# Gathering expert rows with one transfer per slot or with two, in a transformer kernel on one core

## Chip, core and metric

The kernel runs on 1 core of a Trainium2 chip. The metric is the device time of one execution in microseconds (us), taken as the median of several runs. Durations below come from one profiled execution; in the profile PE is TensorE's matmuls and PEld its weight loads, DVE is VectorE, ACT ScalarE, POOL GpSimd and SP SyncE.

## What is computed

The kernel computes two transformer blocks for 512 tokens of width 1024. The stage that matters is the expert layer of the first block. Each token picks 8 heads x 16 = 128 experts out of 16384; for each it takes a row of 1024 floats of a table u and one of a table v:

```python
ug = jnp.take(u_tab, idx, axis=0)
act = jax.nn.gelu(jnp.einsum('td,thkd->thk', xb, ug).astype(jnp.float32), approximate=False)
vg = jnp.take(v_tab, idx, axis=0)
return jnp.einsum('thk,thkd->td', (gate * act).astype(xb.dtype), vg)
```

Before it stand a recurrent mixer and the query projection, behind it a gated feed-forward, attention with a second mixer, and a second feed-forward. They are not touched.

## The kernel before, in words

The 512 tokens are 4 tiles (TT) of 128 tokens, one token per partition. One of a token's 128 chosen experts is a **slot**, so a tile has 128 slots and the layer 512. The work runs slot by slot through five engines, with a ring of 8 row buffers (GROUPS = 8); 8 slots are a round, and a tile has 16 rounds.

Before the change the two tables lie side by side as one table `peer_uv` of 16384 rows of 2048 floats (8 KB). For a slot:

1. GpSimd issues one indirect DMA (L2006) that fetches for each of the 128 tokens the 8 KB row that its expert index names: 1 MB, 128 rows. The indices come from a small tile `expert_ids`, which GpSimd copies out of the index tensor every 16 slots (L1997). Ahead of every second slot, `hold` (L110) makes GpSimd wait on the semaphore `used`, which TensorE raises when it is done with a slot; after an index copy it waits for the copy, and once per half tile for the routing. The transfer raises `uv_in[b]` for buffer b.
2. VectorE waits for `uv_in[b]` and takes the dot product of the u half with the token's activations (L2351, both inputs in SBUF, fused multiply and sum); between rounds it works on pieces of the routing (top-k) of the next tile (`route`, L2263 on), on a schedule written out by hand.
3. ScalarE applies gelu (L2155), multiplies by the gate (L2157), and scales an identity matrix with it (L2160), which gives a diagonal matrix of weights.
4. TensorE waits for that matrix and for `uv_in[b]`, multiplies it with the v half (L2065: two matmuls of 512 columns in the program, four records in the trace) into the tile's sum in PSUM, and raises `used`.

Buffer 0 is `uv_spare`, buffer 1 the upper half of `h2` (shown as `h`), the others `uv_rows`. When a tile is full, ScalarE stores the sum, and TensorE turns it back and adds it to x while the next tile runs; for the last tile this stands at the end of the stage. TensorE, VectorE and ScalarE each have their queue in program order, and GpSimd's queue in this stage holds only the index copies, the waits and the indirect DMAs. SP's queue loads weights and issues nothing in the slots.

Of the kernel before, what the change touches and what calls it, by code (L numbers as in the profile page):

```python
# [1852 lines left out]
GROUPS = 8  # L1853
ROUND = SLOTS_IN_GROUP * GROUPS
ROUNDS = SLOTS // ROUND
# [14 lines left out]
BACK_TURN, BACK_SUM, BACK_ADD, BACK_SQUARE, BACK_ROOT, BACK_SCALE = 7, 11, 9, 10, 13, 14  # L1870


def experts(nc, w, x, weight, keys, consts, uv_tab, norm_after):

# [10 lines left out]
    with ExitStack() as ctx:  # L1887
        signal = Signals(nc, ctx)
# [25 lines left out]
        with ExitStack() as first:  # L1914
# [7 lines left out]
        uv = [uv_spare[:, :, :], h2[:, 4:8].rearrange("p (a k) t -> p a (k t)", a=2), uv_late[:, 0], uv_late[:, 1],  # L1922
              *(uv_late[:, 3 + j] for j in range(4))]
        u, v = [rows[:, 0] for rows in uv], [rows[:, 1] for rows in uv]
        ids = sb("expert_ids", 2, ID_SLOTS, dt=U32)
# [22 lines left out]
        scored0, copied0, scored, copied, routed, shifted, exped, own = map(signal, (  # L1948
            "first_scores", "first_copied", "scores_ready", "scores_copied", "tile_routed", "gate_shifted",
            "gate_exped", "route_own"))  # L1950
        uv_in = [signal(f"uv_rows_in{b}") for b in range(GROUPS)]
        dots, gelus, weights, diagonals, used, ids_out, tile_done, tile_out, zeroed, pace_p = map(signal, (
            "dots_ready", "gelus_ready", "weights_ready", "diagonals_ready", "rows_used", "ids_laid_out",
            "tile_summed", "tile_stored", "zero_ready", "pace_pool"))
# [30 lines left out]
        @block.gpsimd  # L1985
        def _(pool):
            for k in range(0, KD, 2):
                nc.gpsimd.tensor_tensor(sq[:, k], x[:, k], x[:, k], ALU.mult).then_inc(squared_p, 1)
            halves = 2
            per_half = ID_SLOTS // SLOTS_IN_GROUP  # L1990
            turns = SLOTS // (2 * halves * ID_SLOTS)
            with pool.Fori(0, 2 * TT) as ht:
                hold(pool, routed, ht + 2, pace_p)
                with pool.Fori(0, turns) as r:
                    for b in range(halves):
                        n = ht * (turns * halves) + r * halves + b
                        nc.gpsimd.tensor_copy(ids[:, b], idx[:, :, :].rearrange("p t s -> p (t s)")[:, DS(n * ID_SLOTS, ID_SLOTS)]  # L1997
                                              ).then_inc(ids_out, 1)
                        hold(pool, ids_out, n + 1, pace_p)
                        for k in range(per_half):  # L2000
                            if k % 2 == 0:
                                hold(pool, used, n * per_half + k + 2, pace_p)
                            first = k % GROUPS * SLOTS_IN_GROUP
                            for j in range(SLOTS_IN_GROUP):
                                at = k * SLOTS_IN_GROUP + j
                                nc.gpsimd.indirect_dma_start(  # L2006
                                    out=uv[first + j].rearrange("p a d -> p (a d)"), out_offset=None, in_=uv_tab,
                                    in_offset=bass.IndirectOffsetOnAxis(ap=ids[:, b, at:at + 1], axis=0)
                                ).then_inc(uv_in[k % GROUPS], 16)

        @block.tensor
        def _(pe):
# [46 lines left out]
            def sum_rounds(t, first, end):  # L2059
                with pe.Fori(first, end) as r:  # L2060
                    for b in range(GROUPS):
                        pe.wait_ge(diagonals, r * GROUPS + (t * SLOTS + b + 1))
                        pe.wait_ge(uv_in[b], (r + (t * ROUNDS + 1)) * 16)
                        for half in range(2):
                            mm = nc.tensor.matmul(total[:, t % 2, half], diag[:, b], v[b][:, half * T:(half + 1) * T],  # L2065
                                                  start=False, stop=False)
                        mm.then_inc(used, 1)
# [175 lines left out]
        def _(dve):  # L2243
            a = nc.vector
# [102 lines left out]
            def dot_round(t, r):  # L2347

                for b in range(GROUPS):
                    dve.wait_ge(uv_in[b], (r + 1) * 16)  # L2350
                    a.tensor_tensor_reduce(out=u[b], in0=u[b], in1=h_tok[:, t], scale=1.0, scalar=0.0,  # L2351
                                           op0=ALU.mult, op1=ALU.add, accum_out=dot[:, b:b + 1]).then_inc(dots, 1)

# [602 lines left out]
def build(nc, io):  # L2956
    out = io["out"]
    line = io["bias_line"]
    lines = nc.dram_tensor("bias_lines", [8 * P, line.shape[1]], F32).ap()
    saved = [nc.dram_tensor(f"{n}_kept", [P, PAIRS * T], F32).ap() for n in ("gate", "bonus", "pool")]  # L2960
    x_in = io["x"].rearrange("p (k t) -> p k t", k=KD)

    with ExitStack() as whole:
        const_sb = whole.enter_context(nc.sbuf_tensor("const_sb", [P, N_CONST], F32))
        vec_sb = whole.enter_context(nc.sbuf_tensor("vec_sb", [P, N_VEC], F32))

        def consts(name):
            at, n = C_AT[name]
            return const_sb[:, at:at + n]

        def vec(name):
            at, n = V_AT[name]
            return vec_sb[:, at:at + n]

        x = whole.enter_context(nc.sbuf_tensor("x", [P, KD, T], F32))
        load(nc, "start", (vec_sb[:, :], io["vec"]))
        with ExitStack() as s1:
            ar = s1.enter_context(nc.sbuf_tensor("ar", [P, 2, 2, PAIRS, T], F32))
            with ExitStack() as early:
                bk = early.enter_context(nc.sbuf_tensor("bk", [P, 2, 2, PAIRS, T], F32))  # L2980
                v = early.enter_context(nc.sbuf_tensor("v_kept", [P, PAIRS, T], F32))
                w_end = early.enter_context(nc.sbuf_tensor("w_end", [P, 2, NCHUNK, PAIRS], F32))
                front(nc, io, x, x_in, const_sb[:, :], consts, vec, ar, bk, v, w_end, saved)
                o = ar[:, :, 0]
                kept = [src.rearrange("p (a t) -> p a t", a=PAIRS) for src in saved]
                first = OutFirst(nc, early, io["w_out"], kept[2])
                recurrence(nc, ar, bk, v, w_end, consts, o, line, lines, first)
                gate, bonus = (early.enter_context(nc.sbuf_tensor(f"{n}_again", [P, PAIRS, T], F32)) for n in ("gate", "bonus"))
                spread_sb = early.enter_context(nc.sbuf_tensor("head_spread_again", [P, P], F32))
                saved_in = [(gate[:, :, :], kept[0]), (bonus[:, :, :], kept[1]), (spread_sb[:, :], io["head_spread"])]  # L2990
                mixer_out(nc, o, x, vec("lnw"), vec("lnb"), consts, saved_in, gate, bonus, spread_sb, first)

        experts(nc, io["peer_wq"], x, vec("norm2"), io["peer_keys"], consts, io["peer_uv"], vec("norm_f"))
        kept = ahead_tensors(nc, whole, "ahead", AHEAD)
        mix, branches, ffn2_in = (Ahead(*kept, io[name], AHEAD) for name in ("w_in_2", "w_branches", "ffn2_w_in"))
        swiglu_ffn(nc, "ffn1", x, vec("n1"), consts, io["ffn1_w_in"], io["ffn1_w_out"], None, mix)
        with ExitStack() as s3:
            def sb(name, shape, dt=F32):
                return s3.enter_context(nc.sbuf_tensor(name, shape, dt))

            pr = sb("pr", [P, N_IN2, T])
            mixer_in(nc, io["w_in_2"], x, vec("n2"), consts, pr, io["rope"], lines, mix, branches)
            oa, ob = pr[:, C_QA:C_QA + PAIRS], pr[:, C_QB:C_QB + PAIRS]
            merged = pr[:, C_GA:C_GA + KD, :]
            w_out2 = Ahead(*ahead_tensors(nc, s3, "w_out2_ahead", 6), io["w_out_2"], 6)
            with ExitStack() as s0:
                a_parts, b_parts = parts(nc, s0, "oa", PAIRS), parts(nc, s0, "ob", PAIRS)
                gemm(nc, "branches", io["w_branches"], PAIRS, [Operand(*a_parts, oa), Operand(*b_parts, ob)], 2 * KD,
                     Merge(merged, pr), None, branches, w_out2)
            m_parts = parts(nc, s3, "merged", KD)  # L3010
            gemm(nc, "w_out2", io["w_out_2"], KD, [Operand(*m_parts, merged)], KD, AddTo(x), None, w_out2, ffn2_in)
        swiglu_ffn(nc, "ffn2", x, vec("n3"), consts, io["ffn2_w_in"], io["ffn2_w_out"], ffn2_in, None,
                   (vec("nf"), out.rearrange("p (k t) -> p k t", k=KD)))
# [67 lines left out]
def _layout(inp):  # L3081
    a = {k: np.asarray(v) for k, v in inp.items()}
    one = {k: v[0] for k, v in a.items() if v.ndim > 1}
# [17 lines left out]
        "w_out": _blocks(one["w_out"]),  # L3101
        "peer_wq": _blocks(one["peer_wq"]),
        "peer_keys": one["peer_keys"].transpose(3, 0, 1, 2).reshape(P, -1),
        "peer_uv": np.concatenate([one["peer_u"], one["peer_v"]], axis=1),
    }
    for f in ("ffn1", "ffn2"):
        w = one[f"{f}_w_in_2"].reshape(D, 2, KF, P).transpose(0, 2, 1, 3).reshape(D, 2 * D_FF)
# [2 lines left out]
    w = one["w_in_2"]  # L3110
# [27 lines left out]
```

## Time and profile before

| | us |
|---|---|
| median of 3 runs | 3085.91 |
| lowest and highest run | 3078.45, 3086.03 |
| the profiled execution: its time | 3082.82 |
| the profiled execution: span from first to last instruction | 3080.6 |
| busy in the span: TensorE matmuls | 2701.1 |
| busy: VectorE | 1808.7 |
| busy: ScalarE | 1107.3 |
| busy: GpSimd | 779.6 |

The busy times are sums over the whole span. The expert layer's slots fill the stretch from about 525 to about 1834 us, some four tenths of it, so a share over the whole span says little about it: the rows below are read for that stretch.

### The profile page before, as it was taken

What the parts mean: (1) busy time and instruction counts of PE and PEld (TensorE: products, weight loads), DVE (VectorE), ACT (ScalarE), POOL (GpSimd) and SP (SyncE); (2) the same over time, 40 slices, a digit from 0 to 9 for tenths busy, and PEclk for the clock granted to TensorE, in tenths of its full rate; (3) what the DMA queues carried; (4) which work ended last, traced back from release to release, by engine and by line L of the source; (5) the groups of instructions that cost most, each with busy time, mean ns of one, the idle gap of its engine ahead of it and who ended that gap; (6) DMA issues with size and microseconds to landing.
All of it is one profiled execution on the core that took longest, in us unless ns stands there. A gap on an engine that the chain in (4) does not pass through costs nothing. (4 is left out here: it accounts for less than half of the span.)

```text
span 3080.6 us, 41375 instructions
## 1 busy us (share of the span) xinstructions
PE 2701.1 (88%) x14406; PEld 1723.9 (56%) x14406; DVE 1808.7 (59%) x3526; ACT 1107.3 (36%) x2573; POOL 779.6 (25%) x658
## 2 busy tenths in 40 slices
PE   8979999877787788778877879999999999899998
PEld 6669768322232333323322227887766676678876
DVE  6966568666766666666644546443276744554432
ACT  5622232434433443343433333221135455322221
POOL 0311011544545455544555530000010000100000
PEclk9989999999999899999999999999999999999999
DMA  4220123999999999999999973223131112232231
GB/s 151 65 85 4 45 89 122 418 401 411 405 403 421 411 417 403 421 415 416 407 421 420 421 304 108 91 93 123 38 117 58 61 61 62 79 102 95 89 126 46
DMA packets 117168, 679.59 MB, mean 221 GB/s; under 512 B 12968, under 2 KB 16296, under 8 KB 49448
## 3 DMA queue, kind: packets, MB, share of 16 engines
q0 software_dynamic: 73728, 536.90, 42.3%
q1 hardware_dynamic: 42152, 138.76, 13.5%
q10 hardware_dynamic: 1152, 2.10, 0.2%
q8 instruction: 87, 1.43, 0.2%
q14 instruction: 49, 0.40, 0.0%
HBM read 672.47 MB, written 7.86 MB: 221 GB/s over the span
## 5 line engine op out<-in xcount | busy, mean ns | idle before, releaser
L2065 PE MATMUL expert_total<-uv_rows,h 128*128 128x512 f32 x1536 | 725.7, 607 | 110.8 <-ACT h L2160 110.1
L2351 DVE CUSTOM_DVE_ANT_0 uv_rows<-uv_rows,h_tok 128x1024 f32<-128x1024 f32 x384 | 469.6, 1226 | 421.7 <-DMA uv_rows<-in_peer_uv,expert_ids 421.5
L2065 PEld LDWEIGHTS expert_total<-uv_rows,h 128*128 128x128 f32 x1536 | 273.0, 189 | 557.6 <-ACT h L2160 307.8
L2006 POOL DMA_INDIRECT uv_rows<-in_peer_uv,expert_ids x384 | 488.5, 1272 | 336.8 <-PE expert_total L2065 248.8
L2155 ACT ACTIVATE expert_acts<-expert_dots 128x1 f32<-128x1 f32 x512 | 103.7, 203 | 672.6 <-DVE expert_dots L2351 667.9
L293 PE MATMUL ffn_in_out<-ffn_h_hi,ffn_in_w_hi 128*128 128x512 f32 x702 | 281.3, 401 | 12.8 <-DVE ffn_in_w_lo L380 12.8
L2065 PE MATMUL expert_total<-uv_spare,h 128*128 128x512 f32 x256 | 161.5, 764 | 141.4 <-ACT h L2160 140.7
L294 PE MATMUL ffn_in_out<-ffn_h_lo,ffn_in_w_hi 128*128 128x512 f32 x702 | 279.6, 398 | 0.0
L295 PE MATMUL ffn_in_out<-ffn_h_hi,ffn_in_w_lo 128*128 128x512 f32 x702 | 279.3, 398 | 0.0
L372 DVE TENSOR_TENSOR ffn_in_w_lo<-ffn_in_w,ffn_in_w_hi 128x1024 fp32r<-128x1024 f32 x86 | 105.3, 1225 | 213.9 <-ACT ffn_in_w_hi L323 213.8
L2160 ACT ACTIVATE h<-const_sb,expert_weights 128x128 f32<-128x128 f32 x512 | 205.5, 401 | 16.7
L323 ACT CAST ffn_in_w_hi<-ffn_in_w 128x1024 fp32r<-128x1024 f32 x86 | 90.2, 1048 | 267.3 <-PE ffn_in_out L295 254.6
L2065 PEld LDWEIGHTS expert_total<-uv_spare,h 128*128 128x128 f32 x256 | 52.1, 224 | 228.4 <-issue 228.4
L2157 ACT ACTIVATE expert_weights<-expert_acts,expert_gate 128x1 f32<-128x1 f32 x512 | 150.8, 295 | 59.6 <-ACT expert_acts L2155 1.7
L293 PEld LDWEIGHTS ffn_in_out<-ffn_h_hi,ffn_in_w_hi 128*128 128x128 f32 x702 | 133.2, 190 | 47.3 <-issue 9.8
L2006 POOL DMA_INDIRECT uv_spare<-in_peer_uv,expert_ids x64 | 83.3, 1302 | 275.8 <-PE expert_total L2065 273.1
L295 PEld LDWEIGHTS ffn_in_out<-ffn_h_hi,ffn_in_w_lo 128*128 128x128 f32 x702 | 133.2, 190 | 32.5
L294 PEld LDWEIGHTS ffn_in_out<-ffn_h_lo,ffn_in_w_hi 128*128 128x128 f32 x702 | 133.3, 190 | 32.3 <-issue 0.5
L2065 PE MATMUL expert_total<-h 128*128 128x512 f32 x256 | 138.1, 666 | 7.7 <-ACT h L2160 7.6
L2583 PE MATMUL mix_out<-h_hi,mix_w_hi 128*128 128x512 f32 x302 | 127.4, 422 | 1.6 <-DVE mix_w_lo L2857 1.6
L2585 PE MATMUL mix_out<-h_hi,mix_w_lo 128*128 128x512 f32 x302 | 119.0, 394 | 0.0
L2584 PE MATMUL mix_out<-h_lo,mix_w_hi 128*128 128x512 f32 x302 | 118.8, 393 | 0.0
(502 smaller groups left out, 4698.0 us busy)
## 6 DMA issues: line engine op xcount, KB each, us to landing
ffn_in_w<-in_ffn_w_in SPq DMA_DIRECT2D x86, 512.0 KB, 3.5
mix_w<-in_w_in SPq DMA_DIRECT2D x39, 512.0 KB, 3.5
ffn_out_w<-in_ffn_w_out SPq DMA_DIRECT2D x7, 1408.0 KB, 6.2
last_w<-in_ffn_w_out SPq DMA_DIRECT2D x7, 1408.0 KB, 6.2
w_in<-in_w_in SPq DMA_DIRECT2D x19, 512.0 KB, 3.5
wq_w<-in_peer_wq SPq DMA_DIRECT2D x15, 512.0 KB, 3.5
uv_rows<-in_peer_uv,expert_ids POOLq DMA_INDIRECT x384, 12.6
w_out_w<-in_w_out SPq DMA_DIRECT2D x16, 256.0 KB, 3.0
```

Source lines behind the costliest of these rows:

```text
L293: nc.tensor.matmul(out[:, b], high, hi[:, k], start=(k == 0), stop=False)
L294: nc.tensor.matmul(out[:, b], high, lo[:, k], start=False, stop=False)
L295: mm = nc.tensor.matmul(out[:, b], low, hi[:, k], start=False, stop=(k == kt - 1))
L372: nc.vector.tensor_tensor(w_lo[:, n % SLOT], raw[:, n % SLOT], w_hi[:, n % SLOT].bitcast(F32), ALU.subtract).then_inc(parted, 1)
L2006: nc.gpsimd.indirect_dma_start(out=uv[first + j].rearrange("p a d -> p (a d)"), out_offset=None, in_=uv_tab, in_offset=bass.IndirectOffset ...
L2065: mm = nc.tensor.matmul(total[:, t % 2, half], diag[:, b], v[b][:, half * T:(half + 1) * T], start=False, stop=False)
L2157: nc.scalar.activation(scale_[:, at], act_[:, at], ACT.Copy, scale=gate[:, :, :].rearrange("p t s -> p (t s)")[:, DS(g, 1)]).then_inc(weig ...
L2160: nc.scalar.activation(diag[:, b], consts("ident"), ACT.Copy, scale=scale_[:, at]).then_inc(diagonals, 1)
L2351: a.tensor_tensor_reduce(out=u[b], in0=u[b], in1=h_tok[:, t], scale=1.0, scalar=0.0, op0=ALU.mult, op1=ALU.add, accum_out=dot[:, b:b + 1]) ...
L2583: nc.tensor.matmul(bank, high, hi[:, k], start=(k == 0), stop=False)
L2584: nc.tensor.matmul(bank, high, lo[:, k], start=False, stop=False)
L2585: mm = nc.tensor.matmul(bank, low, hi[:, k], start=False, stop=(k == KD - 1))
```

## The change

Each slot is fetched by two indirect DMAs from two tables of 4 KB rows, with the same index column, one after the other on GpSimd's queue: first u, then v, each with semaphores of its own. VectorE's dot product waits for u's, TensorE's matmul for v's. The buffers, the ring of 8, the `used` waits and all computation are unchanged. The host no longer joins the tables.

```diff
-def experts(nc, w, x, weight, keys, consts, uv_tab, norm_after):
+def experts(nc, w, x, weight, keys, consts, u_tab, v_tab, norm_after):
...
-        uv_in = [signal(f"uv_rows_in{b}") for b in range(GROUPS)]
+        u_in, v_in = ([signal(f"{n}_rows_in{b}") for b in range(GROUPS)] for n in ("u", "v"))
...
                                 nc.gpsimd.indirect_dma_start(
-                                    out=uv[first + j].rearrange("p a d -> p (a d)"), out_offset=None, in_=uv_tab,
+                                    out=u[first + j], out_offset=None, in_=u_tab,
                                     in_offset=bass.IndirectOffsetOnAxis(ap=ids[:, b, at:at + 1], axis=0)
-                                ).then_inc(uv_in[k % GROUPS], 16)
+                                ).then_inc(u_in[k % GROUPS], 16)
+                                nc.gpsimd.indirect_dma_start(
+                                    out=v[first + j], out_offset=None, in_=v_tab,
+                                    in_offset=bass.IndirectOffsetOnAxis(ap=ids[:, b, at:at + 1], axis=0)
+                                ).then_inc(v_in[k % GROUPS], 16)
...
-                        pe.wait_ge(uv_in[b], (r + (t * ROUNDS + 1)) * 16)
+                        pe.wait_ge(v_in[b], (r + (t * ROUNDS + 1)) * 16)
...
-                    dve.wait_ge(uv_in[b], (r + 1) * 16)
+                    dve.wait_ge(u_in[b], (r + 1) * 16)
...
-        "peer_uv": np.concatenate([one["peer_u"], one["peer_v"]], axis=1),
+        "peer_u": one["peer_u"], "peer_v": one["peer_v"],
```

## Rows read from the trace of the kernel before

**Rows 1.** The page: the span, and GB/s of all transfers in 40 equal slices.

```profile
span 3080.6 us, 41375 instructions
GB/s 151 65 85 4 45 89 122 418 401 411 405 403 421 411 417 403 421 415 416 407 421 420 421 304 108 91 93 123 38 117 58 61 61 62 79 102 95 89 126 46
```

**Rows 2.** Busy time by stretch: PE, PEld, DVE, ACT, POOL; then clock, DMA share, GB/s.

```profile
524.00:1840.00 1316.00, 1051.61 (x2300) 415.78 (x2298) 830.37 (x1866) 521.15 (x1606) 659.32 (x543) 0.95 0.99 408
```

**Rows 3.** Waits in 524 to 1840 us: us in total, times, longest.

```profile
DVE uv_rows L2351 <- DMA uv_rows<-in_peer_uv,expert_ids: 421.5, 344, 2.2
POOL uv_spare L2006 <- PE expert_total L2065: 273.1, 61, 11.1
POOL uv_rows L2006 <- PE expert_total L2065: 248.8, 145, 3.1
```

**Rows 4.** The page's DMA queues (packets, MB, share) and issues (count, us to landing).

```profile
q0 software_dynamic: 73728, 536.90, 42.3%
...
uv_rows<-in_peer_uv,expert_ids POOLq DMA_INDIRECT x384, 12.6
```

**Rows 5.** Line L2006: count, ns min/median/max, first and last start.

```profile
L2006 POOL DMA_INDIRECT uv_rows<-in_peer_uv,expert_ids x384: 932/940/1993, 528.0 to 1816.1; - x192
L2006 POOL DMA_INDIRECT uv_spare<-in_peer_uv,expert_ids x64: 936/1174/1888, 524.9 to 1802.2; - x64
```

**Rows 6.** Timeline of POOL, 1601 to 1811 us: start, us, and idle time before.

```profile
1805.60 0.94 POOL L2006 DMA_INDIRECT uv_rows<-in_peer_uv,expert_ids  x1 [0.32 <-issue]
1806.84 0.94 POOL L2006 DMA_INDIRECT uv_rows<-in_peer_uv,expert_ids  x1 [0.30 <-issue]
...
1617.36 1.28 POOL L2006 DMA_INDIRECT uv_rows<-in_peer_uv,expert_ids  x1 [1.20 <-issue]
1618.64 0.21 POOL L1997 COPY expert_ids<-expert_idx 128x16 uint32 x1
1619.83 1.33 POOL L2006 DMA_INDIRECT uv_spare<-in_peer_uv,expert_ids  x1 [0.98 <-POOL expert_ids L1997]
```

**Rows 7.** Timeline of POOL and of DVE, 1802 to 1811 us.

```profile
1802.16 1.88 POOL L2006 DMA_INDIRECT uv_spare<-in_peer_uv,expert_ids  x1 [4.35 <-PE expert_total L2065]
1809.58 1.94 POOL L2006 DMA_INDIRECT uv_rows<-in_peer_uv,expert_ids  x1 [1.80 <-PE expert_total L2065]
...
1802.00 1.23 DVE L2351 CUSTOM_DVE_ANT_0 uv_rows<-uv_rows,h_tok 128x1024 f32<-128x1024 f32 x1 [1.26 <-DMA uv_rows<-in_peer_uv,expert_ids]
1806.99 1.23 DVE L2351 CUSTOM_DVE_ANT_0 uv_rows<-uv_rows,h_tok 128x1024 f32<-128x1024 f32 x1 [1.26 <-DMA uv_rows<-in_peer_uv,expert_ids]
1809.49 1.22 DVE L2351 CUSTOM_DVE_ANT_0 uv_rows<-uv_rows,h_tok 128x1024 f32<-128x1024 f32 x1 [1.26 <-DMA uv_rows<-in_peer_uv,expert_ids]
```

**Rows 8.** Groups in 524 to 1840 us: busy us, mean ns, idle before.

```profile
L2006 POOL DMA_INDIRECT uv_rows<-in_peer_uv,expert_ids x384 | 488.5, 1272 | 336.8 <-PE expert_total L2065 248.8 <-issue 84.7 <-ACTq L2202 3.2
...
L2326 DVE TENSOR_TENSOR cands<-cand_partf,const_sb 128x1024 f32<-128x1024 f32 (+1 forms) x16 | 16.8, 1088 | 0.3
L2330 DVE TENSOR_TENSOR cands<-cands,key_idxf 128x1024 f32<-128x1024 f32 (+1 forms) x16 | 16.7, 1087 | 0.1
```

**Rows 9.** The DMA view of 2000 to 2100 us: queue of 4 KB rows, and its issues.

```profile
q1 hardware_dynamic: 2304, 8.39, 25.2%
...
ffn_in_w<-in_ffn_w_in SPq DMA_DIRECT2D x16, 512.0 KB, 3.4
```

**Rows 10.** Timeline of the last slot: its dot product and its matmuls.

```profile
1829.41 1.23 DVE L2351 CUSTOM_DVE_ANT_0 uv_rows<-uv_rows,h_tok 128x1024 f32<-128x1024 f32 x1 [1.25 <-DMA uv_rows<-in_peer_uv,expert_ids]
...
1831.69 1.98 PE L2065 MATMUL expert_total<-uv_rows,h 128*128 128x512 f32 x4 [0.49 <-ACT h L2160]
```

**Rows 11.** Busy time where the clock is lowered (columns as in rows 2); line L2065.

```profile
1065.00:1070.00 5.00, 1.51 (x4) 0.38 (x2) 4.97 (x23) 0.78 (x2) 2.29 (x3) 0.97 1.03 428
1070.00:1075.00 5.00, 3.80 (x5) 1.74 (x6) 3.78 (x7) 3.59 (x12) 0.00 (x0) 0.50 1.01 419
...
L2065 PE MATMUL expert_total<-uv_spare,h x256: 592/650/1218, 539.5 to 1817.7; 128*128 128x512 f32 x128
```

More of the change, by code:

```diff
@@ L2991, in build @@
                 mixer_out(nc, o, x, vec("lnw"), vec("lnb"), consts, saved_in, gate, bonus, spread_sb, first)
-        experts(nc, io["peer_wq"], x, vec("norm2"), io["peer_keys"], consts, io["peer_uv"], vec("norm_f"))
+        experts(nc, io["peer_wq"], x, vec("norm2"), io["peer_keys"], consts, io["peer_u"], io["peer_v"], vec("norm_f"))
         kept = ahead_tensors(nc, whole, "ahead", AHEAD)
```

## The prediction

> **What bounds the kernel now.** I read the page's slices first. From slice 8 to slice 23 the transfers run at 401 to 421 GB/s, elsewhere mostly far below [rows 1]: one stage lives on its transfers. The view by stretch says the same of that stage: from 524 to 1840 us the DMA engines are busy 0.99 of the time, while TensorE is busy 1052 of 1316 us, VectorE 830, GpSimd 659 [rows 2]. The waits confirm it. VectorE waits 421.5 us for rows to land, and GpSimd waits 273 + 249 us for TensorE to free a buffer [rows 3]: GpSimd, which starts the transfers, has time to spare, and each transfer needs 12.6 us to land because it stands in a full queue [rows 4]. The first indirect DMA starts at 524.9, the last at 1816.1 [rows 5]; 511 intervals in 1291 us are 2.53 us per slot. The queue's own share gives the same: 42.3% of 3080.6 us over 512 slots is 2.55 us of every DMA engine per slot [rows 1, 4]. So a slot costs what its 1 MB costs, and no wait on VectorE can make it cheaper.
>
> **What the change touches.** The bytes stay; GpSimd's instructions double, from 512 to 1024. So I price a slot on GpSimd's queue.
>
> *Bare issue.* One indirect DMA takes 0.94 us of GpSimd, and the next starts 0.30 us later when nothing holds it [rows 6]: 1.24 us. Each fetches 128 rows, whether of 8 KB or of 4 KB. That the 0.94 us does not shrink with the row is my choice: the count of rows stays, and the trace has no indirect DMA with a shorter row. The bounds are 0.94 (goes by rows) and 0.47 (goes by bytes). Two cost 2.48 us per slot, just short of the 2.53 that a slot takes now.
>
> *Index copies.* From the end of a DMA at 1618.64 to the next start at 1619.83 are 1.19 us instead of 0.30 [rows 6]; 0.89 us per 16 slots is 0.06 per slot, unchanged, but no longer hidden in waiting.
>
> *Lock against VectorE.* The median issue takes 0.94 us, the mean 1.27 [rows 5, 8]. The timelines side by side show why. The DMA at 1802.16 begins 0.16 us into a dot product that ends at 1803.23, and ends at 1804.04; that at 1809.58 meets one that ends at 1810.71, and ends at 1811.52. Both end 0.81 us after the dot product [rows 7]. The DMA at 1806.84 starts 0.15 us before a dot product and takes its bare 0.94 [rows 6, 7]. So a DMA that begins while a dot product runs waits for its end; one that is 0.15 us ahead is free. The Trainium skill says this of the port ("SBUF — State Buffer", section "Who interferes with whom"): a VectorE instruction with two SBUF inputs contends with a GpSimd instruction that reads SBUF. By that rule, the trace agrees. Today this costs nothing, since GpSimd waits for `used` anyway.
> After the change each slot has one dot product of 1.23 us and two DMAs 1.24 us apart, so nearly every dot product catches one of them, and delays it by 0 to 1.2 us, 0.61 if the phase is even. Once per round VectorE works on routing: (830 - 512 x 1.23) / 64 is 3.1 us [rows 2, 7], after which a late dot product runs right behind another; there a freed DMA keeps step and loses only about 0.06. With one such in eight the mean is 7/8 x 0.61 + 1/8 x 0.06 = 0.54 us. The 32 large two-input operations of the routing [rows 8] cost as much each: 32 x 0.54 / 512 = 0.03.
>
> *Is the phase even?* A 512 KB load lands 3.4 us after its issue [rows 9]; with the 0.94 of GpSimd, u lands some 4.3 us after its DMA began, and its dot product starts then. Call the slot period L = 2.54 + x, x the delay. If the dot product falls between the next slot's u and v DMA, 4.3 = L + 0.12 + x, x = 0.82; if behind its v DMA, 4.3 = L + 1.36 + x, x = 0.20. Both patterns hold themselves up, at L = 3.39 and 2.77 with the routing's 0.03. Index copies and routing throw the kernel from one into the other. Their mean, 3.08, is near the even phase, which I take.
>
> *DMA engines.* Twice as many packets, half as long. Bounds: the present rate (2.55 us per slot) and the 4 KB rows of isolated weight loads, 25.2% of 100 us for 16 loads of 512 KB, 1.58 us each, two of them 3.15 [rows 9]. A queue that is fed every 1.5 us is nearer the first. Either is hidden beside GpSimd, if only just at the upper end.
>
> *Semaphores.* VectorE waits for u alone. v is issued 1.24 to 2.5 us behind u; the matmuls need the diagonal matrix first, 2.28 us after the dot product starts [rows 10]. So TensorE rarely waits for v. It needs 1.98 us per slot [rows 10], below 3.1. Ahead of every second slot four DMAs now queue behind the wait for `used`, but at 3.1 us a ring of eight is 25 us, against 4.3 + 2.3 + 2.0 = 8.6 from issue to free, so that wait ends early. SP's queue is not passed.
>
> *Ends.* Now the last slot's dot product starts 13.35 us after its DMA began (1829.41 less 1816.06) [rows 5, 10], later 4.3: 9 us back. The start of the stage is alike.
>
> **Sum.** 2.48 + 0.06 + 0.54 + 0.03 = 3.11, rounded up to 3.12 for stray waits. 511 x 3.12 = 1594; less 1291 is +303; less 9 is **+294 us**. On the profiled execution (3082.8, span 3080.6) that gives 3377; the median of the runs stands 3.1 higher: 3380.
>
> **The rivals.**
>
> *Issue is cheap, the DMA engines stay the bound (8%).* If generation goes by bytes, GpSimd needs 2 x (0.47 + 0.30) + 0.06 + 0.57 = 2.17 us per slot, below 2.55. Then only the packets can cost: taken at 2.60, near the full queue, 511 x 2.60 less 1291 is +38, and the time 3122. Against it: 0.94 us in every bare issue, the same for all three buffers. The Trainium skill speaks for it ("DMA: Bandwidth & Descriptors", section "Issuing engines are not separate DMA queues"): the time to initiate a DMA is usually small relative to the DMA itself. Here the trace has 1.24 us beside 2.55, so it disagrees.
>
> *Not slower (3%).* The same mechanism, with 4 KB rows moving at today's rate. It decides from the point where generation falls below about 0.65 us (2 x 0.95 + 0.63 = 2.53). Then the u wait gains half a row's transfer once, at the end of the stage: 3085.9 - 1.3 = 3084.6.
>
> *The phases evade the lock (10%).* DMAs and dot products settle so that little is lost: L between 2.60 and 2.75, 3115 to 3191. For it: the second pattern above is near. Against it: at such an L the DMA queue fills, u lands later, and x grows.
>
> *TensorE's clock falls, or the lock is worse (9%).* In 1070 to 1075 us the granted clock is 0.50, the 1.2 GHz level; in the 5 us before, TensorE was busy for 1.5, and single matmuls take up to 1218 ns instead of 592 [rows 11]. TensorE would have 1.1 us of idle per slot instead of 0.5. At half clock a slot takes 2 x 1.98 = 3.96 us: over the whole stage 3810. A dot product that cost its full 1.2 us every time would give L = 3.8 and 3728. Against it: with stalls for lack of work already, the clock is 0.95 on average [rows 2], so this can cost a fraction of that at most.
>
> **How the numbers follow.** The forecast's case (GpSimd bound, L 2.77 to 3.39) has 70%: 3202 to 3518. The first two rivals and a third of the third are left out below, half of the fourth above. The range is 3140 to 3510. A measurement of this kernel can tell 0.3%, 9 us, from no change. Faster by more would need slots below 2.51 us on engines that are 0.99 busy: 1%. Within it: 3%. Slower: 96%.
>
> **What would show it.** In the new profile: 1024 indirect DMAs, median 0.94 us, mean 1.2 to 1.3; GpSimd busy about eight tenths of the stage with idle time that is "issue", not TensorE; issue to landing down from 12.6 to 4 or 5 us; 320 to 350 GB/s; the last indirect DMA near 2120 us. A median far below 0.94, or a DMA share still at 0.99, would prove me wrong; so would GpSimd still waiting for TensorE.

## The result and the profile after

| | before | after |
|---|---|---|
| median, us | 3085.18 | 3263.20 |
| lowest and highest, us | 3078.45, 3086.03 | 3255.62, 3264.27 |
| profiled execution, us | 3082.82 | 3264.27 |
| its span, us | 3080.6 | 3262.5 |

The ratio is 1.0579, with a 95% interval from 1.0566 to 1.0591: slower by 178 us, where 294 were forecast.

The page of the changed kernel: the slices of the expert stage, and the queue of its transfers.

```profile
span 3262.5 us, 41887 instructions
GB/s 149 62 74 4 58 94 215 349 357 363 365 353 376 346 372 350 367 355 374 359 352 386 366 368 261 97 96 77 139 72 65 58 65 51 85 94 90 96 119 51
q0 software_dynamic: 147456, 536.94, 44.1%
```

The bytes are the same 536.9 MB, in twice as many packets. The plateau of 401 to 421 GB/s [rows 1] has come down to 346 to 386.

The view by stretch over the whole stage (PE, PEld, DVE, ACT, POOL, then clock, DMA share, GB/s), and the view of the tile of indices, which has both indirect DMAs (count, ns min/median/max, first and last start):

```profile
524.00:2020.00 1496.00, 1079.01 (x2311) 412.31 (x2309) 835.37 (x1873) 522.07 (x1608) 1147.15 (x1056) 0.96 0.96 359
```

```profile
L2006 POOL DMA_INDIRECT uv_rows<-in_peer_u,expert_ids x384: 933/938/1992, 532.8 to 2004.9; - x192
L2010 POOL DMA_INDIRECT uv_rows<-in_peer_v,expert_ids x384: 933/1002/1992, 534.0 to 2006.2; - x192
L2006 POOL DMA_INDIRECT uv_spare<-in_peer_u,expert_ids x64: 934/964/1949, 527.6 to 1986.4; - x64
...
  PE expert_total L2069: 17.8, 32
...
DMA to landing us min/median/max: 4.5/6.2/7.8
```

GpSimd is now busy 1147 of 1496 us; before it was 659 of 1316 [rows 2]. It waited 273 + 249 us for TensorE to free buffers [rows 3]; that has shrunk to 17.8 us. The bare issue is still 0.93 to 0.94 us, with rows half as long [rows 5]. From the first u issue at 527.6 to the last at 2004.9 are 511 intervals of 2.891 us, where they were 2.527. A transfer lands after 6.2 us instead of 12.6 [rows 4]: the transfer queue is no longer full, GpSimd's is. The mean of all 1024 issues is 1.108 us, where 0.938 is bare. The account closes: 511 x 0.364 is +186 us; the stage starts 2.7 us later; and at the end the last dot product starts 5.9 us after its DMA began instead of 13.35, 7.5 us back. Together +181, and the spans differ by 182.

The two queues side by side, in a stretch of the last tile (start, us, and idle time before):

```profile
1955.08 0.99 POOL L2010 DMA_INDIRECT uv_rows<-in_peer_v,expert_ids  x1 [0.30 <-issue]
...
1957.62 1.97 POOL L2010 DMA_INDIRECT uv_rows<-in_peer_v,expert_ids  x1 [0.30 <-issue]
...
1954.04 1.23 DVE L2355 CUSTOM_DVE_ANT_0 uv_rows<-uv_rows,h_tok 128x1024 f32<-128x1024 f32 x1 [1.30 <-DMA uv_rows<-in_peer_u,expert_ids]
1957.56 1.23 DVE L2355 CUSTOM_DVE_ANT_0 uv_rows<-uv_rows,h_tok 128x1024 f32<-128x1024 f32 x1 [2.29 <-DMA uv_rows<-in_peer_u,expert_ids]
```

The idle time before each of these DMAs is 0.30 us and named "issue": GpSimd never rests here. The dot product of 1954.04 costs the v DMA of 1955.08 only 0.05 us, since it ends 0.19 us after that DMA has begun. The one of 1957.56 begins 0.06 us ahead of a DMA and holds it to 1.97 us, which ends 0.80 us after the dot product, as in [rows 7]. Over the stage, the DMAs that end 0.81 us after a dot product are 421, and they take 151 us longer than bare ones, 0.29 us per slot. The 32 DMAs behind the index copies take 11 us longer, and those behind the routing's two-input instructions most of the rest, to 0.34 us per slot in all.

### The profile page after: what moved, and what is told of

It is laid out like the page before. It is cut to its first block and busy times, and to the rows that moved or that the text cites. A ratio compares the mean times of both kernels' runs of the same rounds, so it can differ in the third digit from the quotient of the medians.

```text
span 3262.5 us, 41887 instructions
## 1 busy us (share of the span) xinstructions
PE 2728.6 (84%) x14406; PEld 1719.4 (53%) x14406; DVE 1809.9 (55%) x3526; ACT 1108.6 (34%) x2573; POOL 1265.4 (39%) x1170
## 3 DMA queue, kind: packets, MB, share of 16 engines
q0 software_dynamic: 147456, 536.94, 44.1%
## 5 line engine op out<-in xcount | busy, mean ns | idle before, releaser
L2069 PE MATMUL expert_total<-uv_rows,h 128*128 128x512 f32 x1536 | 743.5, 613 | 232.4 <-ACT h L2164 229.9
L2010 POOL DMA_INDIRECT uv_rows<-in_peer_v,expert_ids x384 | 437.2, 1139 | 117.1 <-issue 114.6
L2006 POOL DMA_INDIRECT uv_rows<-in_peer_u,expert_ids x384 | 414.8, 1080 | 117.1 <-issue 115.3
L2069 PE MATMUL expert_total<-uv_spare,h 128*128 128x512 f32 x256 | 168.4, 793 | 163.4 <-ACT h L2164 162.7
```

What stands on the lines that cost most here:

```text
L2006: nc.gpsimd.indirect_dma_start(out=u[first + j], out_offset=None, in_=u_tab, in_offset=bass.IndirectOffsetOnAxis(ap=ids[:, b, at:at + 1], ...
L2010: nc.gpsimd.indirect_dma_start(out=v[first + j], out_offset=None, in_=v_tab, in_offset=bass.IndirectOffsetOnAxis(ap=ids[:, b, at:at + 1], ...
```

## The experiments

Two theories. **A**: GpSimd's queue sets the slot time, by the bare issue of two DMAs and by the waits behind two-input VectorE instructions. **B**: the DMA engines set it, because 4 KB rows move slower. B had something to go on: the DMA share after is still 0.96, near the 0.99 that the prediction named as a sign against it, and 44.1% of 16 x 3262.5 us over 131072 rows is 0.176 us per row, or 2.81 us of every engine per slot.

### Take away the lock: a dot product with one SBUF input

```diff
-                    a.tensor_tensor_reduce(out=u[b], in0=u[b], in1=h_tok[:, t], scale=1.0, scalar=0.0,
-                                           op0=ALU.mult, op1=ALU.add, accum_out=dot[:, b:b + 1]).then_inc(dots, 1)
+                    a.tensor_reduce(dot[:, b:b + 1], u[b], AX.X, ALU.add).then_inc(dots, 1)
```

On the changed kernel:

> The changed kernel with the dot product replaced by a plain sum of the u row (a VectorE reduction with one SBUF input; the product with the token's activations is left out). Theory A (GpSimd's issue plus the waits behind two-input VectorE instructions set the slot time): mean indirect DMA back to 0.94 to 0.96 us, slot period 2.54 to 2.62 us instead of 2.89, time 3085 to 3130. Theory B (the DMA engines set it, because 4 KB rows move slower: 0.175 us x 16 = 2.80 us per slot): the shorter issue changes nothing, slot period 2.80 or more, time 3215 to 3263.

Measured: 3105.63 us, ratio 1.0069 (1.0052 to 1.0086). Its view of the index tile and by stretch:

```profile
L2006 POOL DMA_INDIRECT uv_rows<-in_peer_u,expert_ids x384: 933/937/1742, 531.3 to 1843.3; - x192
L2010 POOL DMA_INDIRECT uv_rows<-in_peer_v,expert_ids x384: 933/937/1991, 532.5 to 1844.6; - x192
L2006 POOL DMA_INDIRECT uv_spare<-in_peer_u,expert_ids x64: 932/950/1137, 526.1 to 1825.9; - x64
```

```profile
524.00:1850.00 1326.00, 1052.81 (x2282) 416.68 (x2281) 820.03 (x1353) 517.68 (x1598) 975.19 (x1056) 0.94 1.02 405
```

Both medians are bare, the mean of all 1024 is 0.945 us, and the period is (1843.3 - 526.1) / 511 = 2.58 us. VectorE is about as busy, 820 us against 835, so it is not its time that was in the way. The edit takes away two things at once, the second input and the 1024-column output that the dot product writes to SBUF. The trace of the changed kernel tells them apart. Beside the dot products stands an addition of the same length, with the same output in SBUF, whose one input is in SBUF and the other in PSUM (`score_out`):

```profile
1142.48 1.23 DVE L2360 TENSOR_TENSOR x<-score_out,x 128x1024 f32<-128x1024 f32 x1
1143.11 0.94 POOL L2006 DMA_INDIRECT uv_rows<-in_peer_u,expert_ids  x1 [0.30 <-issue]
```

The DMA that begins inside it takes its bare 0.94 us. So do the three others that begin at least 0.15 us before the end of this addition in the kernels before and after, at 0.93 to 0.94 us. The DMAs that begin so inside the routing's TENSOR_TENSOR instructions with both inputs in SBUF (L2305, L2330 and L2334, 22 DMAs in the changed kernel) take 1.41 us in the mean, and none less than 0.97. It is the second SBUF input that holds a DMA, not the output.

The same 4 KB rows now move at 405 GB/s. B falls as the cause of the loss: the kernel is 158 us faster with the same rows, and the time per row is 0.165 us (43.5% of 16 x 3106.3 us over 131072) instead of 0.176. Of the 178 us the lock accounts for about 158; the 22 us that this run still stands above the kernel before, measured beside it, fit the bare issue and the packets, which at 2.58 us stand level: GpSimd 975 us busy plus 0.30 per DMA, DMA share 1.02.

The control is the same edit on the kernel before:

> The kernel before with the same plain sum in place of the dot product; it is the control of the run above. Both theories: GpSimd had time to spare and the DMA queue was full, so the indirect DMAs shrink from 1.26 to about 0.94 us and the time stays within 0.3% of the kernel before, 3076 to 3095.

3077.47 us, ratio 0.9979 (0.9970 to 0.9989): without the lock the joint transfers gain 0.2%, though their DMAs shrink from a mean of 1.257 to 0.956 us. In the kernel before, the lock was there in full and was hidden by the wait for buffers.

### Double the issues, leave the rows

```diff
+                                nc.gpsimd.indirect_dma_start(
+                                    out=tiny[:, first + j], out_offset=None, in_=tiny_tab,
+                                    in_offset=bass.IndirectOffsetOnAxis(ap=ids[:, b, at:at + 1], axis=0)
+                                ).then_inc(tiny_in[k % GROUPS], 16)
```

> The kernel before with its 8 KB rows, plus a second indirect DMA per slot of 64 B rows into a scratch tile (16 floats of the same expert, used by nothing; TensorE waits for it). Theory A: 1024 issues as in the changed kernel, slot period about 2.9 us, time 3230 to 3290. Theory B: rows move as fast as before plus some 0.1 us of small packets per slot, time 3085 to 3140.

3261.99 us (3250 to 3279), ratio 1.0576 (1.0529 to 1.0622): the changed kernel's time within the spread of the runs.

```profile
L2013 POOL DMA_INDIRECT tiny_rows<-in_peer_tiny,expert_ids x512: 940/975/1992, 524.2 to 2011.9; - x171
L2009 POOL DMA_INDIRECT uv_rows<-in_peer_uv,expert_ids x384: 939/944/1991, 528.0 to 2010.7; - x192
```

A DMA of 64 B rows occupies GpSimd as long as one of 8 KB rows, 0.94 us. The loss comes with the number of instructions; a part of the split rows in it is too small to be seen here.

### Halve the rows of an issue

Neither run says whether 0.94 us goes by the 128 rows or by the instruction. Two DMAs of 64 partitions for each joint slot:

```diff
+                                for half in (slice(0, P // 2), slice(P // 2, P)):
...
-                                    out=uv[first + j].rearrange("p a d -> p (a d)"), out_offset=None, in_=uv_tab,
-                                    in_offset=bass.IndirectOffsetOnAxis(ap=ids[:, b, at:at + 1], axis=0)
+                                        out=uv[first + j].rearrange("p a d -> p (a d)")[half], out_offset=None, in_=uv_tab,
+                                        in_offset=bass.IndirectOffsetOnAxis(ap=ids[0:P // 2, b, at:at + 1], axis=0)
```

> The kernel before with its joint 8 KB rows, each slot fetched by two indirect DMAs of 64 partitions (the second uses the row indices of tokens 0 to 63 again, so tokens 64 to 127 get rows that are not theirs). Instructions double, rows and bytes stay. If an issue costs by its rows: 0.47 to 0.55 us each, GpSimd keeps time to spare, time 3080 to 3110. If it costs by the instruction (0.94 us each, whatever its rows): slot period about 2.9 us, time 3230 to 3290.

4137.84 us, ratio 1.3327 (1.3257 to 1.3396): neither expectation. Its view of line L2007, and its DMA queue:

```profile
L2007 POOL DMA_INDIRECT uv_rows<-in_peer_uv,expert_ids x768: 891/897/1952, 532.7 to 2873.3; - x192
...
  PE expert_total L2066: 952.1, 245
```

```profile
GB/s 130 80 17 54 92 200 223 224 224 225 225 226 225 225 226 227 228 236 234 233 229 229 230 229 229 229 229 194 94 93 114 62 86 59 59 82 85 95 111 62
...
q0 software_dynamic: 81920, 536.94, 58.1%
```

The run answers the question by the duration of its issues: half the rows cost 0.897 instead of 0.937 us. So nearly all of an issue is fixed, 0.86 us by these two points, and a row adds 0.6 ns. Its time has another cause. GpSimd waits 952 us for buffers again, because the transfers run at 223 to 236 GB/s: a row of 8 KB takes 0.59 us (58.1% of 16 x 4147.5 us over 65536 rows) where 42.3% of 16 x 3080.6 made 0.32 [rows 1, 4]. The Trainium skill has this in "SBUF — State Buffer", section "Door 1: The DMA port swizzle": a transfer into partitions 0 to 63 reaches 8 of the 16 ports. By that rule the rate halves; the trace agrees, with both halves in one queue. That this is the cause was not tested further; the run also fetches the rows of tokens 0 to 63 twice.

### Halve the bytes, leave the issues

```diff
-                                    out=v[first + j], out_offset=None, in_=v_tab,
+                                    out=tiny[:, first + j], out_offset=None, in_=tiny_tab,
...
-                            mm = nc.tensor.matmul(total[:, t % 2, half], diag[:, b], v[b][:, half * T:(half + 1) * T],
+                            mm = nc.tensor.matmul(total[:, t % 2, half], diag[:, b], u[b][:, half * T:(half + 1) * T],
```

> The changed kernel with v's 4 KB rows replaced by 64 B rows into a scratch tile (TensorE multiplies the u half in v's place, so the output leaves out v). Issues as in the changed kernel, half the bytes. If the DMA engines set the slot time in the changed kernel: much faster, below 3085. If GpSimd does, and the delay depends on where the dot product falls among the issues: u lands after 4.3 instead of 6.1 us, the delay is 0.8 us (slot period 3.39) or 0.2 us (2.77) or a mix of the two, so 3200 to 3510 and likelier slower than the changed kernel's 3263, with half the data. If the delay does not depend on the landing time: slot period 2.89, 3263.

3281.69 us, ratio 1.0637 (1.0619 to 1.0655). The changed kernel ran beside it on the same chip:

> The changed kernel as it is, for comparison with the other runs of this call: 3255 to 3270. If the wait for both transfers in place of u alone was truly faster, this run stands about 15 us above its 3248.

3254.13 us, ratio 1.0556 (1.0539 to 1.0574). With half the data the stage is slower. The view by stretch of the kernel with the tiny v, and its time from issue to landing:

```profile
524.00:2045.00 1521.00, 1091.52 (x2291) 415.53 (x2289) 831.78 (x1865) 520.18 (x1605) 1177.68 (x1055) 0.95 0.62 179
```

```profile
DMA to landing us min/median/max: 3.1/4.2/5.6
```

The DMA engines are busy 0.62 of the time and move 179 GB/s, yet a slot takes (2034.1 - 524.8) / 511 = 2.95 us (last and first start of u's DMAs). Transfers land after 4.2 us (u's alone after 4.4), the 4.3 that the prediction had used; in the changed kernel it is 6.2. The mean issue is 1.133 us instead of 1.101 in the changed kernel beside it; the bare one is 0.943 instead of 0.937. That the early landing makes the worse phase is what the prediction's two patterns say (0.8 or 0.2 us); measured were 0.38 per slot, below the middle of the two.

### Wait for both transfers

```diff
                     dve.wait_ge(u_in[b], (r + 1) * 16)
+                    dve.wait_ge(v_in[b], (r + 1) * 16)
```

> The changed kernel with VectorE waiting for v as well as u: the split transfers without the early start. If the early start of VectorE is worth nothing in a stage bound elsewhere: 3255 to 3270. Theory A with its phases: the dot product moves about 1.3 us later against GpSimd's issues, so the mean delay changes from 0.34 us per slot to something between 0.3 and 0.75, slot period 2.86 to 3.27, time 3250 to 3460. Theory B: no change, 3263.

3248.47 us, ratio 1.0540 (1.0523 to 1.0558), below the changed kernel's 1.0579 and just below all that was expected. The changed kernel measured once more, above, had 3254.13, only 6 us more, so both ran again side by side on one chip:

> The changed kernel with VectorE waiting for u and v once more, beside the changed kernel on the same chip: 3240 to 3260. If the early start is worth nothing the two agree within 0.3%.

> The changed kernel once more, for the comparison: 3250 to 3265.

3252.68 us, ratio 1.0556 (1.0539 to 1.0572), against 3248.78, ratio 1.0542 (1.0518 to 1.0567). The intervals overlap. The early start of VectorE, the one thing the second transfer was to buy, cannot be measured. Part of it turns up as waiting of TensorE, which is seen in who waited for v's DMA (us and times): in the changed kernel

```profile
  PEld expert_total L2069: 193.8, 54
```

and with the wait for both, in the first of its runs

```profile
  PEld expert_total L2069: 49.0, 13
```

### Move the dot product

```diff
                     dve.wait_ge(u_in[b], (r + 1) * 16)
+                    a.tensor_reduce(filler[:, b:b + 1], h_tok[:, t, 0:T], AX.X, ALU.add)
```

> The changed kernel with a VectorE sum over 512 columns of the activations (one SBUF input, about 0.55 us, its result used by nothing) between the wait for u and the dot product. It moves each dot product later by 0.6 us against GpSimd's issues. Phase theory: dot product 6.8 instead of 6.2 us after the issue, so the delay is (6.8 - 5.2) / 3 = 0.5 us instead of 0.3, slot period 3.1, time 3320 to 3380. Without a part for the phase: VectorE has room for it (54% busy), time 3255 to 3275.

3270.38 us, ratio 1.0596 (1.0564 to 1.0627), against 1.0556 for the changed kernel on the same chip. The intervals overlap, and the time is the one expected without a part for the phase. The phase theory's number falls: a delay of 0.36 us per slot (mean issue 1.117), not 0.5. Counting in the trace how many DMAs have begun, by at least 0.06 us, between a slot's u DMA and its dot product suggests why. In the changed kernel the commonest count is 4 (287 of 512 dot products), and there the dot product starts a median 0.36 us after the latest DMA began. With the filler the counts 4 and 5 have 188 and 187. With 4 the median is 0.63 us, about as the equation has it (0.12 + 0.5); with 5 it is 0.23. The pushed dot products fall behind the next DMA, where they cost little.

### Split every second slot

```diff
+                                if k % 2:
+                                    nc.gpsimd.indirect_dma_start(
+                                        out=uv[first + j].rearrange("p a d -> p (a d)"), out_offset=None, in_=uv_tab,
+                                        in_offset=bass.IndirectOffsetOnAxis(ap=ids[:, b, at:at + 1], axis=0)
+                                    ).then_inc(u_in[k % GROUPS], 16)
+                                    continue
...
-                        pe.wait_ge(v_in[b], (r + (t * ROUNDS + 1)) * 16)
+                        pe.wait_ge((u_in if b % 2 else v_in)[b], (r + (t * ROUNDS + 1)) * 16)
```

> Every second slot split into u and v, the others fetched jointly in 8 KB rows: 1.5 indirect DMAs per slot. GpSimd then needs 1.5 x 1.24 + 0.06 + 0.3 to 0.6 = 2.2 to 2.5 us per slot, just below the 2.55 of the DMA engines, so by theory A most of the loss is gone: 3085 to 3120. A cost that went by the number of split slots would leave half of it: 3165 to 3180.

3111.19 us, ratio 1.0089 (1.0073 to 1.0105): 27 us, about a sixth of the 164 us that the changed kernel lost on the same chip, for half of the split slots. Its stretch view:

```profile
524.00:1840.00 1316.00, 1009.96 (x2272) 420.36 (x2271) 819.94 (x1851) 516.00 (x1583) 893.13 (x796) 0.95 1.00 403
```

The mean issue is 1.155 us, longer than in the changed kernel, but GpSimd has waits for buffers again (165 us) and the DMA engines are full. The bottleneck turns between the two kernels: 1.5 issues per slot fit under 2.55 us, 2 do not.

## Why the prediction was right, and where its size was off

- **What bounds the kernel now.** Right. Taking the lock off the kernel before, which took 0.30 us off the mean issue, gave 0.2%.
- **Bare issue, 2.48 us.** Right in its number: the bare 0.94 and 0.30 are in the profile after. The reason chosen for it, that it goes by rows, was wrong. It goes by the instruction, which was not among the bounds. The term came out right only because the change leaves 128 rows to each issue.
- **Index copies, ends.** 0.06 us stands as it was worked out, within the rest of the period: 2.891 less 2 x 0.938, 2 x 0.305 and 0.34 leaves 0.065. The end gave 7.5 us back, not 9, since u lands later than assumed.
- **Lock against VectorE.** The mechanism is shown (158 us go with the second SBUF input). Its size is the term that failed: 0.54 + 0.03 us per slot were forecast, 2 x (1.108 - 0.938) = 0.34 measured. That is 0.23 x 511 = 118 us, about all of the 117 us by which 3380 exceeds 3263.2. Nearly every dot product was to hold a DMA, for 0.61 us in the mean; 421 DMAs were held by one, for 0.36 us in the mean.
- **The step inside it.** The landing time of 4.3 us came from an isolated load; in the changed kernel it is 6.2. The prediction's equations then have another pattern, with one more slot to share the delay: 6.2 = 2L + 0.12 + x with L = 2.54 + x gives x = 0.33. The measured delay is 0.34 and the period 2.89. But this agreement may be luck, since the same equation gave 0.5 for the run with the filler, which had 0.36. Nor is the landing time the whole of it: in the run with the tiny v it was 4.4 us, as the prediction had it, and the delay was 0.38. Over five kernels with two issues per slot and the two-input dot product the delay was 0.27 to 0.38 us, with landing times of u from 4.4 to 6.3. So taking the mean of the two patterns, the even phase, overstated the delay in all of them. In the changed kernel the phases are far from even: of 512 dot products 182 begin between 0.06 and 0.26 us after a DMA began, where an even spread over the mean 1.44 us between DMAs would have 71. With the tiny v they are 96, against 69. What holds the phases there stays open; it was not settled by these runs.
- **DMA engines.** Right that they are hidden; the 3.15 us bound was far off. The full queue moves 4 KB rows at 405 GB/s. In the changed kernel they land after 6.2 us and move at 359 GB/s, where 4 to 5 us and 320 to 350 GB/s were forecast.
- **Semaphores.** VectorE's early start is worth nothing measurable, as forecast. That TensorE rarely waits for v was right in times (54 of 512), though those waits are long.
- **Rivals.** "Issue is cheap" falls by the medians, "not slower" with it. "The phases evade the lock" was half true: the period of 2.89 lies between it and the forecast. TensorE's clock did not fall: 0.96 over the stage, 0.95 before [rows 2]. The wide range, 3140 to 3510, held both patterns of the phase; it would not have told the lock's size from half of it.

## What to carry to other kernels

An instruction that an idle engine issues is free only up to that engine's slack, and the slack is to be counted with its waits: here GpSimd's 0.94 + 0.30 us per indirect DMA, twice, plus 0.34 of lock, against 2.53 us per slot. Price a split of a transfer by the number of issues, not by bytes or rows, and ask first whether the wait that it shortens is the one that ends the stage; in a stage whose DMA engines are 0.99 busy, no earlier semaphore helps. Once a second engine comes level with the first, its hidden stalls (here behind two-input VectorE instructions) all come into the open.

## What was not expected of the hardware

- An indirect DMA costs GpSimd 0.897 us for 64 rows of 8 KB, 0.937 for 128 rows of 8 KB or of 4 KB, and 0.94 for 128 rows of 64 B: close to a fixed price.
- It waits for a running VectorE instruction if that has two SBUF inputs, and here for no other: in the first experiment 484 DMAs began while the 1024-column sum with one input ran, and took 0.938 us in the mean and 0.97 at most, and the four inside the addition with one input in PSUM took 0.93 to 0.94 in the kernels before and after.
- Two DMAs of 64 partitions halved the transfer rate of the stage, from about 410 to about 227 GB/s.
- Half the bytes made the stage slower (2.95 instead of 2.88 us per slot, side by side). Most of it is a longer lock (0.38 instead of 0.33 us per slot) as the rows land earlier; 0.01 is the bare issue. No run isolates the landing time.
